# A decoder trunk step on one core: one ring buffer for mixers and experts, with eight gathers issued in front of the stage barrier

## The reference, cut to what matters

```python
def block(xb):                       # xb: normalised rows, D = 1024
    q = (xb @ wq).reshape(T, 8, 2, 128)
    s = einsum('thpd,pkd->thpk', q, subkeys)
    ...                              # top 16 of 16x16 pair sums for each of 8 heads
    idx = take_along_axis(cidx, sel) # 8 x 16 = 128 experts of 16384 for each token
    g = softmax(top_s)
    u = u_tab[idx]                   # 128 rows of 1024 for each token
    act = gelu(einsum('thkd,td->thk', u, xb))
    vv = v_tab[idx]                  # 128 more rows for each token
    return einsum('thk,thkd->td', g * act, vv)
```

## Time and profile before

| what | value |
|---|---|
| median of 3 runs | 1992.82 us |
| lowest and highest | 1985.81, 1994.36 us |
| the profiled execution, its own time | 1993.35 us |
| its span in the trace | 1991.6 us |
| mean granted TensorE clock | 0.917 |
| PE, DVE, POOL, ACT busy | 79%, 61%, 54%, 23% |
| moved by DMA | 713.42 MB, mean 358 GB/s |

### The profile page before, as it was taken

One profiled execution on the slowest core, in us unless ns is written; L12 is line 12 of the kernel. 1 busy time (PEld: TensorE's weight loads), 2 busy tenths in 40 slices (PEclk: granted clock), 3 DMA queues, 4 the chain that ended last, 5 costly groups with the idle time before them and its releaser, 6 DMA issues.

```text
span 1991.6 us, 17753 instructions
## 1 busy us (share of the span) xinstructions
PE 1577.7 (79%) x5461; PEld 734.6 (37%) x5461; DVE 1212.3 (61%) x3132; ACT 466.6 (23%) x1212; POOL 1083.7 (54%) x1168
## 2 busy tenths in 40 slices
PE   6989989898558467778788888888889889799943
PEld 1524546554126113223343333333344344354410
DVE  2123265868778701115767776777676688879973
ACT  1131312122101111212221322222232232322421
POOL 3000011222543445777777777777767777677774
PEclk9999999898765688998999999999999899999976
DMA  9696667697995799999999999999999999999997
GB/s 328 228 365 215 230 227 274 230 386 168 399 378 204 254 412 368 396 412 387 390 419 419 420 419 419 420 419 420 419 391 416 392 411 419 391 411 417 418 371 269
DMA packets 237564, 713.42 MB, mean 358 GB/s; under 512 B 23101, under 2 KB 49055, under 8 KB 237456
## 3 DMA queue, kind: packets, MB, share of 16 engines
q0 software_dynamic: 156672, 570.49, 72.6%
q1 hardware_dynamic: 80488, 140.73, 19.8%
q10 hardware_dynamic: 312, 1.07, 0.2%
HBM read 704.42 MB, written 8.25 MB: 358 GB/s over the span
## 4 chain that ended last, share of the span: by engine, by line
DMA 17%; PE 15%; POOL 14%; DVE 12%; issue 6%; ACT 2%; POOLq 0%; ACTq 0%; DVEq 0%
DMA v_rows<-in_peer_v_dram,expert_idx_ring 10%; PE ps_y L2373 8%; POOL u_rows L1932 6%; DVE u_rows L2152 6%; POOL v_rows L1938 6%; DMA v_rows<-in_peer_v_dram,tile_idx 5%; PE ps_r L2347 4%; POOL v_rows L1946 2%; PE ps_y L2401 2%; DMA u_rows<-in_peer_u_dram,expert_idx_ring 1%; ACT wt_diag L2043 1%; DVE key_scores_w L2163 1%; DVE top_i L2165 1%; DVE top L2164 0%; PE ps_r L2364 0%
## 5 line engine op out<-in xcount | busy, mean ns | idle before, releaser
L2373 PE MATMUL ps_y<-v_rows,wt_diag 128*128 128x512 f32 x1536 | 731.3, 609 | 136.9 <-DMA v_rows<-in_peer_v_dram,expert_idx_ring 113.1
L2152 DVE CUSTOM_DVE_ANT_0 u_rows<-u_rows,ps_y 128x1024 f32<-128x1024 f32 x360 | 422.7, 1216 | 110.1 <-DMA u_rows<-in_peer_u_dram,expert_idx_ring 109.3
L2373 PEld LDWEIGHTS ps_y<-v_rows,wt_diag 128*128 128x128 f32 x1536 | 272.9, 191 | 534.3 <-issue 479.4
L1932 POOL DMA_INDIRECT u_rows<-in_peer_u_dram,expert_idx_ring x384 | 367.2, 956 | 138.2 <-issue 97.4
L1938 POOL DMA_INDIRECT v_rows<-in_peer_v_dram,expert_idx_ring x384 | 367.3, 956 | 118.1 <-issue 100.1
L615 PE MATMUL ps_z<-w_stream,hT 128*128 128x512 f32 (+5 forms) x560 | 247.3, 599 | 25.6 <-DVE hT L791 15.5
L346 POOL DMA_INDIRECT low_rows<-in_peer_u_dram,tile_idx x128 | 127.3, 995 | 238.0 <-DVE tile_dots L333 153.5
L2401 PE MATMUL ps_y<-v_rows,wt_diag 64*64 64x512 f32 x1024 | 136.4, 651 | 60.5 <-DMA v_rows<-in_peer_v_dram,tile_idx 57.0
L1946 POOL DMA_INDIRECT v_rows<-in_peer_v_dram,tile_idx x128 | 122.3, 956 | 77.6 <-PE ps_y L2401 50.4
L615 PEld LDWEIGHTS ps_z<-w_stream,hT 128*128 128x128 f32 (+1 forms) x560 | 100.8, 184 | 150.6 <-issue 121.0
L2162 DVE MAX8 top<-key_scores 128x8 f32<-128x128 f32 x64 | 18.2, 284 | 179.6 <-ACT key_scores L2023 179.6
(11 more groups left out here) (444 smaller groups left out, 1758.1 us busy)
## 6 DMA issues: line engine op xcount, KB each, us to landing
w_stream<-in_w_in_dram SPq DMA_DIRECT2D x25, 2048.0 KB, 11.7
w_stream<-in_ada_w_dram SPq DMA_DIRECT2D x12, 2048.0 KB, 13.0
w_stream<-in_peer_wq_dram SPq DMA_DIRECT2D x8, 1024.0 KB, 8.4
wq<-in_peer_wq_dram SPq DMA_DIRECT2D x4, 2048.0 KB, 42.5
w_stream<-in_w_in_dram SPq DMA_DIRECT2D x5, 1568.0 KB, 8.4
w_stream<-in_w_in_dram SPq DMA_DIRECT2D x5, 1536.0 KB, 17.1
u_rows<-in_peer_u_dram,expert_idx_ring POOLq DMA_INDIRECT x384, 10.5
v_rows<-in_peer_v_dram,expert_idx_ring POOLq DMA_INDIRECT x384, 11.0
```

The costliest lines, as they stand in the source:

```text
L1932: g.indirect_dma_start(u_rows[:, j, :], None, U, bass.IndirectOffsetOnAxis(where[:, j:j + 1], 0))\
L2152: v.tensor_tensor_reduce(u_rows[:, j, :], u_rows[:, j, :], row[:, :], 1.0, 0.0, ALU.mult, ALU.add, dots[:, par, j:j + 1]).then_inc(s["u_us ...
L2373: mm = nc.tensor.matmul(ps_y[:, c * 512:(c + 1) * 512], diag[:, par, j, :], v_rows[:, j, c * 512:(c + 1) * 512], start=(first and j == 0), ...
```

## The change

The mixers' ring `low_rows` and the experts' ring `v_rows` become one buffer, allocated outside both stages, with the eight landing semaphores of the first ring (`Ahead.u_in`) kept for the second. They are no longer cleared at the end of the first stage, so every wait of the second stage on a v row counts on from V_IN = 16 x 16 = 256. The first eight v gathers of tile 0 are no longer issued by the second stage's POOL program; they stand at the end of the first stage's POOL program, behind its last u gathers, and each waits for the dot that used its slot (`a_used` 121 to 128).

```diff
+    def first_v_gather(self, pool, V, j):
+        pool.wait_ge(self.s["a_used"], PH * TOPK - NB + j + 1)
+        self.nc.gpsimd.indirect_dma_start(self.rows[:, j, :], None, V,
+                                          bass.IndirectOffsetOnAxis(self.keep["idx0"][:, j:j + 1], 0)).then_inc(self.u_in[j], 16)
...
-        self.low = sb("low_rows", [P, NB * D])
+        self.low = rows
...
         A.gathers(pool, U, "sample", "O")
         A.gathers(pool, U, "sample", "Z")
+        for j in range(NB):
+            A.first_v_gather(pool, I["peer_v"][0], j)
...
-        u_rows, v_rows = sb("u_rows", [P, NB, D]), sb("v_rows", [P, NB, D])
+        u_rows, v_rows = sb("u_rows", [P, NB, D]), rows[:, :].rearrange("p (j d) -> p j d", d=D)
...
-        v_in = [ctx.enter_context(nc.semaphore(f"v_in{j}")) for j in range(NB)]
+        v_in, V_IN = rows_in, 16 * GPT
...
-                    if i:
-                        pool.wait_ge(s["v_used"], k + 1 - NB)
+                    pool.wait_ge(s["v_used"], k + 1 - NB)
...
-                for i in range(GPT - 1):
+                for i in range(1, GPT - 1):
                     for j in range(NB):
                         v0_gather(i, j)
...
-                        pe.wait_ge(v_in[j], i * 16 + 16)
-                        pe.wait_ge(v_in[j + 1], i * 16 + 16)
+                        pe.wait_ge(v_in[j], V_IN + i * 16 + 16)
+                        pe.wait_ge(v_in[j + 1], V_IN + i * 16 + 16)
...
+        rows = const("v_rows", [P, NB * D])
...
-        nc.clear_and_free_semaphores([*s.values(), *s2.values(), *X.stream_in, *X.ahead.u_in])
+        nc.clear_and_free_semaphores([*s.values(), *s2.values(), *X.stream_in])
         nc.all_engine_barrier()
-        experts(nc, I, O, mod, x1_dram, K, keep)
+        experts(nc, I, O, mod, x1_dram, K, keep, rows, X.ahead.u_in)
```

More of the change, by code:

```diff
@@ L481, with __init__ @@
 class Mixer:
-    def __init__(self, nc, ctx):
+    def __init__(self, nc, ctx, rows):
         def sb(name, shape, dt=F32):
@@ L1796, with experts @@
 HP = P // 2
-def experts(nc, I, O, mod, x1_dram, K, keep):
+def experts(nc, I, O, mod, x1_dram, K, keep, rows, rows_in):
     with ExitStack() as ctx:
@@ L2370, in sums @@
                         hold(pe, s["diag_ready"], i * NB + (j + 1) + GPT * NB)
-                        hold(pe, v_in[j], i * 16 + 16 + GPT * 16)
+                        hold(pe, v_in[j], V_IN + i * 16 + 16 + GPT * 16)
                         for c in range(2):
@@ L2376, in sums, with sums_smp @@
                         mm.then_inc(s["v_used"], 1)
-                def sums_smp(i, rows=v_rows, landed=v_in, turn=GPT):
+                def sums_smp(i, rows=v_rows, landed=v_in, turn=2 * GPT):
                     for j in range(0, NB, QS):
@@ L2500, in trunk_step @@
             s2["w_out_in"] = s["w_out_in"]
-            X = Mixer(nc, mix)
+            X = Mixer(nc, mix, rows)
             X.stream = Stream(X, s, s2)
```

## The result

Before 1990.58 us (median of 20 runs), after 1997.09 us (20 runs): a ratio of 1.0032 with a 95% interval of [1.002, 1.0044], 6.4 us slower [4.0, 8.8], where 1.1 us less was forecast. The profiled execution took 1994.31 us, its span 1992.6 us.

The account below looks back on a forecast made before the run. The second stage was taken as bound by its transfers: 10.1 us of DMA work removed behind the barrier against a 9.0 us later start gave -1.1 from 1993.35, 1992.2, stated as 1992 us, range 1985 to 1998.

Parts of the forecast that it names:

- At nothing: Whole change: constants added to waits, the buffer's new place and the shorter clearing list were priced at no time.
- partial rival 2: Behind the barrier: the delayed start is paid in part, by the last pair, +0.6 to +5.8, 1994 to 1999; chance 0.13.
- When they are issued: End of first stage on POOL: eight v gathers from 679.5, 1.24 us apart, paced by POOL, not the added wait.
- When the bytes are there: Before the barrier: the eight v gathers' last bytes land at 694.0 us.
- What the barrier then waits for: At the barrier: POOL's drain holds until its gathers land, ending at 695.4; second stage starts 9.0 us later.
- rival 1: At the barrier: the drain does not hold for the v gathers; start 2.7 us later, -7.4, 1986; chance 0.13.
- The sum: Behind the barrier: DMA work shorter by 10.1 us but begun 9.0 later, -1.1; at the far bound +2.0.
- What hides the rest: Start of second stage: SP's loads, 27.5 us, keep the DMA full until group 1 is issued, covering the later PE start.
- rival 2: Behind the barrier: the delayed start is paid through the PE chain; in part 1994 to 1999 (0.13), in full 2002 to 2005 (0.06).
- the dip behind 770 us: Second stage: the DMA share's first dip, to 0.71; its growing with the shift would prove the prediction wrong.

Follow-up runs that it names:

- e13: The change with all eight v gathers of group 0 behind the barrier and the shared ring moved to a multiple of 256 bytes: 1988.69 us, 0.9978 of before.
- e14: The kernel before with only the mixers' ring moved to a multiple of 256 bytes: 1986.65 us, 0.9969 of before.
- e7: The kernel before with `v_rows` allocated as the first buffer of the second stage, only addresses differing: 1.0029 of before.
- e12: The change with the shared ring 64 bytes higher, at a multiple of 256, and 192 unused bytes behind it: 1984.95 us, 0.9967 of before.
- e5: The kernel before run again against itself, as a control: ratio 1.0002.
- e6: The kernel before with only the first ring's landing semaphores kept for the second, both rings at their old places: 1.0009 of before.
- e8: The kernel before with `low_rows` allocated as the first of the mixers' buffers, nothing else changed: 1.0014 of before.
- e1: The change with group 0's eight v gathers issued behind the barrier as before, shared ring and semaphores kept: 1.0029 of before.
- e10: The kernel before with the v ring shifted by a small gap, `wq`, `h_cur` and `u_rows` left where they were: 1.0025 of before.
- e11: The kernel before with `v_rows` allocated right behind `wq`, far from where the change has it: 1.0028 of before.
- e3: The changed kernel run once more, unaltered, on the chip of the other three runs of its round: 1.0024 of before.
- e4: The change with SP issuing the subkeys' load in front of the first rows: 1.002 of before.
- e9: The change with the shared ring shifted a little by gaps, leaving both rings off a multiple of 256: 2014.36 us, 1.0135 of before.
- e15: As e12, with one more gap that puts the mixers' weight buffers at multiples of 256 too: 1976.70 us, 0.9905 of before.
- e17: The kernel of e15 again, on another chip: 1979.32 us, 0.9942 of before.
- e2: The change with only the first two v gathers of group 0 in front of the barrier, the other six behind: 1.0039 of before.

## Why the prediction was wrong

**The step that failed** stands under "At nothing": "the constants added to the waits, the buffer's new place and the shorter list to clear". The constants and the list are at nothing: e13 has both with its ring at a good address, and is 0.9978 [0.9961, 0.9994] where e14 without them is 0.9969 [0.9948, 0.999]. The buffer's new place is not: e7, which has only that, is 1.0029 [1.0008, 1.0049], and with the place mended the change is 0.9967 (e12). The term was priced by instruction counts and by nothing else. With it falls the premise that behind the barrier only idle time of the DMA engines counts: they were as full as before and moved fewer bytes. That the rate of a transfer can hang on where it lands was not among the rivals. The measured 1997.09 lies inside the range of 1985 to 1998 that was given; that is luck, since the upper end had been drawn for the partial rival 2, which nothing here bears out.

Where its cost shows can be read by line: the v gathers of tile 0, first and last start, of before, of e7 and of the change, and the dots of the first stage, whose last start is the second number, of e7 and of the change (before's last dot is in the earlier trace rows):

```profile
L1946 POOL DMA_INDIRECT v_rows<-in_peer_v_dram,tile_idx x128: 932/937/1987, 690.7 to 898.8; - x128
```

```profile
L1947 POOL DMA_INDIRECT v_rows<-in_peer_v_dram,tile_idx x128: 932/937/1646, 687.9 to 897.4; - x128
```

```profile
L1953 POOL DMA_INDIRECT v_rows<-in_peer_v_dram,tile_idx x120: 932/937/1627, 713.0 to 900.7; - x120
```

```profile
L333 DVE CUSTOM_DVE_ANT_0 low_rows<-low_rows,ps_n x71: 1196/1220/1223, 492.8 to 682.4; 128x1024 f32<-128x1024 f32 x71
```

```profile
L333 DVE CUSTOM_DVE_ANT_0 v_rows<-v_rows,ps_n x71: 1197/1219/1223, 496.3 to 687.2; 128x1024 f32<-128x1024 f32 x71
```

Counted from the start of the first stage's last dot (685.2, 682.4 and 687.2) to the last of these gathers it is 213.6, 215.0 and 213.5 us. Traces of one group lie 1 to 5 us apart, so I take all: before, e5, e6 and e8 have 208.9 to 213.6, mean 211.2; e1, e7, e10 and e11, with the v ring off and all gathers behind the barrier, 213.6 to 216.6, mean 215.0: **+3.8 us for the place**, in the one stretch where v rows come alone. (An estimate from the windows gives the same: 128 gathers of 0.524 MB take 160.2 us at 419 GB/s and 164.1 at 409, 3.9 more.) The change, e3, e4 and e9 have 213.3 to 214.6, mean 213.9: **-1.1 us for the barrier**. That this is the sum of the prediction to the tenth is chance, as four single traces on each side don't give tenths. At good addresses it is 211.4 (e12, e15, e17) against 211.2 (seven kernels with all gathers behind): +0.2. So the barrier is worth something between -1.1 and nothing.

**Step by step.** The first stage ends 2.0 us later in the profiled run after than before, so each predicted time counts 2.0 later here.

- *When they are issued*: predicted from 681.5, 1.24 us apart; 681.45 and 1.24. POOL set the pace, not the new wait. Right.
- *When the bytes are there*: predicted 696.0, measured 695.5. Right.
- *What the barrier then waits for*: POOL's drain was predicted to end at 697.4, measured 697.9; SP's first load at 699.1, measured 699.54, 11.2 us behind the last dot's end instead of 1.8, so 9.4 us later (9.0 predicted). Right, and rival 1 is out: the drain does hold until the gathers have landed. The Trainium skill, Perfetto Trace Analysis, section DMA Instruction — SWDGE (GPSIMD), agrees for the gather itself (each record is 0.94 us long, and the last ends at 691.1, 4.4 us ahead of its bytes); it is the drain behind it that waits.
- *The sum*: -1.1, and 10.1 us of DMA time against 9.0 of delay. Measured -1.1 in one comparison and +0.2 in the other. Neither can be told from the other or from nothing; the sum is not contradicted.
- *What hides the rest*: the subkeys reached PE at 708.5, inside 705.9 to 711.1; group 0 took 7.4 us where 10.3 and small gaps were predicted, from pairs that had been slower in before; group 1 was issued at 713.0, inside 711 to 716. Nothing speaks for rival 2: the late PE start costs nothing that e4 could be seen to give back, and the dip behind 770 us has not grown, a share of 0.91 in the 10 us from 772 against 0.71. (The dip's depth says little: in the same 10 us from 770, e5, which is before again, has 0.78, and e6 1.00.)
- *At nothing*: wrong, by +3.8 us where it can be seen.

**What stays open.** The timed loss of the change is 6.4 us [4.0, 8.8]; the traces locate 3.8 - 1.1 = 2.7 of it, or 3.8 if the barrier gains nothing. The kernels with the v ring alone moved lost 5.0 to 5.8 us by the clock (e7, e10 and e11, each with 3 to 4 us to either side), so 3.8 is not too little for the place. From the last v gather of tile 0 to the end of the span it takes 1094.1 us on the mean in before, e5, e6 and e8 and 1094.4 in the eight kernels with the v ring alone off (1114.1 in e9), so no further piece shows behind it, nor ahead of it. Part of the gap may be the scatter of single traces; what the rest is, I can't say.

Why a multiple of 256 matters the runs do not show. The Trainium skill, DMA: Bandwidth & Descriptors, section How a descriptor splits into AXI transactions, has a rule that fits, told there of reads: where a transfer doesn't start at a multiple of 256 bytes, its first transaction starts at the boundary below, and the bytes in front of its start, fetched and not used, still cost. Counted by its table, a row of 4 KB at offset 192 would cost 134 beats instead of 128, an estimate of 4.7% from that page; measured are 409 against 419 GB/s, 2.4%. At offset 64 its estimate is 1.6%, and e10, at 387, loses 8% in this window. So the direction agrees there, the sizes don't; and in the main loop, where the v rows at 192 should cost more by the same rule, the change moves 419 GB/s as before does. By that rule the change would have come out slower, and it belonged among the rivals.

## What to carry to other kernels

A change that merges, adds or reorders buffers moves every buffer behind them: before pricing that at nothing, look where the destinations of the heavy transfers start in the partition before and after, and keep them at multiples of 256 bytes, the only good places among those run. When a stretch is full by its DMA share, read the GB/s beside it too: a share just as full at 2.4% fewer bytes (409 against 419 GB/s) was all that could be seen of the loss here. And to see whether a change's mechanism or its side effects moved the time, run the side effects alone first (e1, e7): one run took the barrier out of suspicion.

## What the runs showed of the hardware

- Gathers of 4 KB rows alone moved some 418 GB/s into a ring at a multiple of 256 bytes, and 387 to 410 at offsets 64, 192 and 224 (20 us windows; 410 and 412 occur at a multiple too); plain loads into a weight buffer 408 to 410 at a multiple, 385 to 388 at offset 224, 387 at 64 (e9).
- Where gathers into two rings alternate, a u ring at a multiple hides the loss of the v ring (419 GB/s); with both off, in the one kernel that has this, it is 409. Why is not known. The issue to landing of a gather in the main loop, median us in the last column, of the change and of e9:

```profile
u_rows<-in_peer_u_dram,expert_idx_ring POOLq DMA_INDIRECT x384, 10.2
v_rows<-in_peer_v_dram,expert_idx_ring POOLq DMA_INDIRECT x384, 10.2
```

```profile
u_rows<-in_peer_u_dram,expert_idx_ring POOLq DMA_INDIRECT x384, 12.6
v_rows<-in_peer_v_dram,expert_idx_ring POOLq DMA_INDIRECT x384, 12.9
```

- POOL's drain at the end of a block ended 2.4 us after the last bytes of its gathers (1.4 and 3.1 in the earlier trace rows), so a gather issued ahead of a barrier held the barrier until it had landed: the second stage began 1.7, 3.3 and 11.2 us behind the last dot with none, two and eight in front (e1, e2 and the change).
